# Writing the weights' low halves over their raw pieces: eight slots for high halves, splits up to six pieces ahead

## The chip, the cores and the metric

The kernel runs on one core of a Trainium2 chip. The metric is the device time of one execution in microseconds (us), the median of several runs. Besides the timed runs there is one execution under the hardware profiler, and every row below is from that one.

## The reference

Two layers of a streaming encoder trunk over 256 positions of width 2048, all in float32. Each layer adds three sub-layers to x, each between two RMSNorms:

```python
x = x + rmsnorm(hybrid_mixer(rmsnorm(x, g[0]), ...), g[1])   # w_in (2048 x 5,000-odd), attention of 16 heads, w_out
x = x + rmsnorm(memory_xattn(rmsnorm(x, g[2]), mem_n, wq_x, wkv_x, wo_x), g[3])
x = x + rmsnorm(conv_ffn(rmsnorm(x, g[4]), w_up, conv_w, conv_b, w_down), g[5])   # w_up 2048 x 8192, w_down 4096 x 2048
```

In the mixer, one part of the projection by w_in is low-rank: `cq` (512 columns) and `ckv` (256 columns and 32 for the rotary key) are each normalized and then multiplied by `w_uq` and `w_ukv` to give queries, keys and values of six heads.

## The kernel before

**The stream of pieces.** All weights of both layers are laid out as one stream of 688 pieces, 344 a layer, each [128 partitions x 1024 float32], 512 KB. A piece is loaded by SP's DMA queue into one of eight slots of `raw`. For TensorE, which is given float32r operands, each piece is split in two parts whose sum is the float32 value: ScalarE (ACT) copies `raw` into `w_hi`, rounded to float32r (`split_hi`, L983), and VectorE (DVE) writes `w_lo = raw - w_hi` (`split_lo`, L1299). TensorE (PE) then multiplies hi by hi, lo by hi and hi by lo into PSUM. `w_hi` and `w_lo` have four slots each (`SPL = 4`). The activations are split likewise (`h_t`, `c_t`, `o_t` and others, by ACT at L991 and DVE at L1331).

**What waits for what.** The semaphores are `landed[slot]` (a load is there), `hi_ready`, `lo_ready` (a split's two halves) and `split_free` (PE has used a piece). ACT's split of piece p waits for the landing and for PE having used piece p - 4. SP's load of piece p + 8 waits for `lo_ready` of piece p, that is until DVE has read the raw piece for the last time. PE's first matmul of a piece waits for `lo_ready` of it.

**The order is written out by hand.** `layer_steps` lists, for the first 152 pieces of a layer and the start of the up-projection, steps such as ("mm", p), ("evac", group), ("latent", "scale"), ("split", q). PE, ACT and DVE each walk through this one list in order and do their part of each step; after the steps of ("mm", p) stands ("split", p + 4). Up- and down-projection are loops with a split for each piece. So an engine that is held at a split is held for all that follows on it.

**The pieces of a layer.** 0 to 7 are `cq` (2 x 512 columns wide), 8 to 15 `ckv` (2 x 288: only 576 columns of the piece are split and multiplied), 16 to 23 `vbf` (2 x 262), 24 to 31 `vb`, 32 and 33 `uqa`, 34 to 37 `small` (the last columns of w_uq and w_ukv; 128 columns), 38 `ukv0`, 39 `ukv1`, 40 to 47 `va`, then 40 pieces of transposed q and k, 32 of w_out, 32 of the cross-attention, 128 of the up- and 64 of the down-projection. A group's result leaves PSUM by its ("evac", group) after its last piece; the groups alternate between two pairs of PSUM banks, so PE's first matmul of a group waits until ACT has emptied the group before the last one.

**The latent chain.** After piece 15 ACT sums the squares of `cq` and `ckv`; after piece 17 DVE computes their rstd; after piece 19 ACT scales them; after piece 20 DVE turns the rotary key; after piece 23 PE transposes two tiles (`latent_T` 0 and 1, L863) into two of four rotating banks, ACT and DVE split them into `c_t`; after piece 24 PE transposes `latent_T` 2, 3 and 4, and number 3 waits for DVE's `c_t` of number 0, which frees its bank. In layer 0 alone DVE also makes six `ind` tiles (L1485) for the bias of the heads of group A in between, and PE multiplies them.

## Time and profile before

| | |
|---|---|
| runs, us | 2049.18, 2048.83, 2047.91; median 2048.83 |
| the profiled execution, us | 2053.52, its span 2051.7 |
| PE busy | 1997.4 us, 97% of the span |
| DVE, ACT busy | 1384.1 us (67%), 1082.1 us (53%) |
| the weights' loads | 688 of 512 KB; DMA engines busy for them 52.2% of the span |
| granted TensorE clock, mean | 0.988 of full speed |

The profiled execution is 1.8 us longer than its span (what lies around the first and the last instruction) and 4.7 us longer than the median of the runs. Busy times count an engine's instructions only; what is left of PE's span, 54.3 us, is idle time: about 14 us of it lie behind its last matmul, and 9.3 us before its third group at the start.

### The profile page before, as it was taken

The numbers are of one execution on the slowest core, as the hardware profiler recorded it, in microseconds if no ns is written. First come the engines' busy times: TensorE is split into PE (matmuls) and PEld (weight loads), VectorE is DVE, ScalarE is ACT, GpSimd is POOL, SyncE is SP. The second block draws the span as 40 slices with busy tenths as digits, with TensorE's granted clock in tenths as the row PEclk, the third lists the DMA queues.
The fourth block names the chain that finished last, engine by engine and source line by source line (L and its number), as shares of the span: only waits on it lengthen the run. The fifth ranks groups of instructions, "written<-read, shape, count | busy, mean of one in ns | idle before, by whom it ended". The sixth has DMA issues, their size and how long they took to land.

```text
span 2051.7 us, 31077 instructions
## 1 busy us (share of the span) xinstructions
PE 1997.4 (97%) x10772; PEld 1710.6 (83%) x10772; DVE 1384.1 (67%) x2141; ACT 1082.1 (53%) x1682; POOL 169.2 (8%) x191
## 2 busy tenths in 40 slices
PE   8999999998999999999989999999989999999997
PEld 6788888887888888888878888788878888888885
DVE  6757676767777777744466576768577777777454
ACT  5665555645555555444456555565555555554442
POOL 0010000000112212100000000000002212211000
PEclk9999999999999999999999999999999999999999
DMA  7664446453555555565547444555445555556552
GB/s 276 219 211 147 163 147 242 176 175 134 178 195 190 182 196 187 183 225 192 192 168 242 165 146 164 186 212 193 149 143 185 186 193 193 181 196 210 193 192 82
DMA packets 104472, 379.00 MB, mean 185 GB/s; under 512 B 12032, under 2 KB 12672, under 8 KB 103040
## 3 DMA queue, kind: packets, MB, share of 16 engines
q1 hardware_dynamic: 101392, 365.11, 52.2%
q10 hardware_dynamic: 2416, 11.14, 1.5%
q0 software_dynamic: 576, 1.57, 0.3%
q8 instruction: 56, 0.92, 0.2%
q14 instruction: 32, 0.26, 0.0%
HBM read 374.90 MB, written 2.88 MB: 184 GB/s over the span
## 4 chain that ended last, share of the span: by engine, by line
PE 94%; DVE 3%; ACT 1%; issue 1%; DMA 0%; SPq 0%; DVEq 0%; ACTq 0%
PE ps L733 23%; PE ps L675 13%; PE ps L677 13%; PE ps L676 13%; PE ps L735 12%; PE ps L688 9%; PE ps L690 5%; PE ps L639 1%; DVE w_lo L1299 1%; DVE x L1443 1%; PE ps L916 1%; PE ps L901 0%; PE ps L904 0%; ACT w_hi L983 0%; PE ps L854 0%
## 5 line engine op out<-in xcount | busy, mean ns | idle before, releaser
L1299 DVE TENSOR_TENSOR w_lo<-raw,w_hi 128x1024 fp32r<-128x1024 f32 (+2 forms) x688 | 816.9, 1191 | 515.8 <-ACT w_hi L983 510.7
L983 ACT ACTIVATE w_hi<-raw 128x1024 fp32r<-128x1024 f32 (+2 forms) x688 | 706.0, 1031 | 493.6 <-PE ps L677 241.0
L733 PE MATMUL ps<-h_t,w_hi 128*128 128x512 f32 x2048 | 716.0, 396 | 4.1 <-DVE h_t L1331 2.4
L735 PE MATMUL ps<-h_t,w_lo 128*128 128x256 f32 x2048 | 569.2, 278 | 0.0
L733 PEld LDWEIGHTS ps<-h_t,w_hi 128*128 128x128 f32 x2048 | 385.9, 188 | 94.3 <-issue 5.2
L735 PEld LDWEIGHTS ps<-h_t,w_lo 128*128 128x128 f32 x2048 | 386.4, 189 | 0.0
L688 PE MATMUL ps<-h_t,w_hi 128*128 128x512 f32 x768 | 275.5, 401 | 0.0
L1787 POOL TENSOR_SCALAR up_c<-up_u,cw 128x256 f32<-128x256 f32 x128 | 125.8, 995 | 1202.0 <-DVE up_u L1682 1202.0
L690 PE MATMUL ps<-h_t,w_lo 128*128 128x256 f32 x768 | 215.2, 280 | 0.0
L675 PE MATMUL ps<-w_hi,act_t 128*128 128x512 f32 x512 | 199.2, 389 | 0.0
L677 PE MATMUL ps<-w_hi,act_t 128*128 128x512 f32 x512 | 199.2, 389 | 0.0
L676 PE MATMUL ps<-w_lo,act_t 128*128 128x512 f32 x512 | 199.2, 389 | 0.0
L688 PEld LDWEIGHTS ps<-h_t,w_hi 128*128 128x128 f32 x768 | 144.2, 188 | 33.6 <-issue 0.7
L690 PEld LDWEIGHTS ps<-h_t,w_lo 128*128 128x128 f32 x768 | 145.1, 189 | 0.3
L675 PE MATMUL ps<-w_hi,h_t 128*128 128x512 f32 (+2 forms) x320 | 117.9, 369 | 3.3 <-DVE w_lo L1299 2.1
L676 PE MATMUL ps<-w_lo,h_t 128*128 128x512 f32 (+2 forms) x320 | 113.7, 355 | 0.0
L677 PE MATMUL ps<-w_hi,h_t 128*128 128x512 f32 (+2 forms) x320 | 113.7, 355 | 0.0
L677 PEld LDWEIGHTS ps<-w_hi,act_t 128*128 128x128 f32 x512 | 96.1, 188 | 20.1
L675 PEld LDWEIGHTS ps<-w_hi,act_t 128*128 128x128 f32 x512 | 96.1, 188 | 20.0
L676 PEld LDWEIGHTS ps<-w_lo,act_t 128*128 128x128 f32 x512 | 96.1, 188 | 19.7
L675 PE MATMUL ps<-w_hi,o_t 128*128 128x512 f32 x256 | 102.9, 402 | 3.0 <-DVE o_t L1331 3.0
L677 PE MATMUL ps<-w_hi,o_t 128*128 128x512 f32 x256 | 100.2, 391 | 0.0
(277 smaller groups left out, 2311.4 us busy)
## 6 DMA issues: line engine op xcount, KB each, us to landing
raw<-stream SPq DMA_DIRECT2D x688, 512.0 KB, 4.0
gain_a<-gains_in ACTq DMA_DIRECT2D x4, 1024.0 KB, 6.6
m_nat<-mem_in ACTq DMA_DIRECT2D x2, 2048.0 KB, 10.6
x<-x_in SPq DMA_DIRECT2D x4, 512.0 KB, 8.1
gain_f<-gains_in ACTq DMA_DIRECT2D x2, 1024.0 KB, 7.7
out<-x SPq DMA_DIRECT2D x4, 512.0 KB, 2.8
bias_hbm<-bias_raw POOLq DMA_DIRECT2D x4, 128.0 KB, 5.1
bias<-bias_hbm POOLq DMA_DIRECT2D x4, 128.0 KB, 7.1
```

What stands on the lines that cost most here:

```text
L639: mm = pe.transpose(b[:, kk * SEQ + tb * P:kk * SEQ + (tb + 1) * P], x[:, tb, (2 * i + kk) * P:(2 * i + kk + 1) * P], ident[:])
L675: pe.matmul(dst, s_hi, hi[:, j, :], start=f, stop=False, skip_group_check=True)
L676: pe.matmul(dst, s_hi, lo[:, j, :], start=False, stop=False, skip_group_check=True)
L677: mm = pe.matmul(dst, s_lo, hi[:, j, :], start=False, stop=e, skip_group_check=True)
L688: pe.matmul(dst, hi[:, j, nt * P:(nt + 1) * P], src[:, c, :, :], start=f, stop=False, skip_group_check=True)
L690: mm = pe.matmul(dst[:, SEQ:2 * SEQ], lo[:, j, nt * P:(nt + 1) * P], src[:, c, 0, :], start=False, stop=e, skip_group_check=True)
L733: pe.matmul(dst, hi[:, cc, nt * P:(nt + 1) * P], h_t[:, c, :, :], start=(c == 0), stop=False, skip_group_check=True)
L735: mm = pe.matmul(dst[:, SEQ:2 * SEQ], lo[:, cc, nt * P:(nt + 1) * P], h_t[:, c, 0, :], start=False, stop=(c == KC - 1), skip_group_check=True)
L916: mm = pe.transpose(b[:, t * P:(t + 1) * P], s_sb[:, slot, o:o + P], ident[:])
L983: act.activation(w_hi[:, slot, 0:width], raw[:, rslot, 0:width], ACT.Copy).then_inc(hi_ready, 1)
L1299: dve.tensor_tensor(w_lo[:, slot, 0:width], raw[:, rslot, 0:width], w_hi[:, slot, 0:width].bitcast(F32), ALU.subtract).then_inc(lo_ready, 1)
L1787: ins = pool.tensor_scalar(up_c[:, nt, :], up_u[:, nt, :], cw[:, 4 * nt + 2:4 * nt + 3], cw[:, 4 * nt + 3:4 * nt + 4], ALU.mult, ALU.add)
```

## The change

Eight slots for `w_hi` take the 32 KB of each partition that four slots of `w_hi` and four of `w_lo` took, and `w_lo` lies at the address of `raw`: DVE writes a piece's low half over the raw piece that it reads in the same instruction. Since the slot of `raw` is then in use until PE has multiplied the piece, SP's load of piece p + 8 waits for `used`, PE's count of used pieces (the old `split_free` under another name and without its start value of 4), instead of `lo_ready` of piece p. ACT's split no longer waits for PE: a landed piece is free to be split, for the load before it has waited already. And the splits stand further ahead in the order: ("split", p + 4) for the first 12 pieces of layer 0, p + 5 up to piece 39, p + 6 from there on and in all of layer 1, so that two steps, after pieces 12 and 40 of layer 0, hold two splits.

```diff
-SPL = 4
+AHEAD = 6
+
+def splits_after(layer, p):
+    if layer > 0:
+        return [p + AHEAD]
+    def target(q):
+        return 3 if q < 0 else q + (4 if q < 12 else 5 if q < 40 else AHEAD)
+    return list(range(target(p - 1) + 1, target(p) + 1))
...
         if p < P_UP - 1:
-            steps.append(("split", p + SPL))
+            steps += [("split", q) for q in splits_after(layer, p)]
...
         raw = sb("raw", [P, RAW, PW], 0)
-        w_hi = sb("w_hi", [P, SPL, PW], 32 * K, F32R)
-        w_lo = sb("w_lo", [P, SPL, PW], 48 * K, F32R)
+        w_hi = sb("w_hi", [P, RAW, PW], 32 * K, F32R)
+        w_lo = sb("w_lo", [P, RAW, PW], 0, F32R)
...
-                    sp.wait_ge(lo_ready, r * RAW + (j + 1 - RAW))
+                    sp.wait_ge(used, r * RAW + (j + 1 - RAW))
                     sp.dma_start(raw[:, j, :], stream[r * RAW + j]).then_inc(landed[j], 16)
...
-            pe.sem_inc(split_free, SPL)
...
-            def split_hi(slot, rslot, landed_count, piece_count, width=PW):
-                act.wait_ge(landed[rslot], landed_count)
-                act.wait_ge(split_free, piece_count)
-                act.activation(w_hi[:, slot, 0:width], raw[:, rslot, 0:width], ACT.Copy).then_inc(hi_ready, 1)
+            def split_hi(slot, landed_count, width=PW):
+                act.wait_ge(landed[slot], landed_count)
+                act.activation(w_hi[:, slot, 0:width], raw[:, slot, 0:width], ACT.Copy).then_inc(hi_ready, 1)
...
-            def split_lo(slot, rslot, count, width=PW):
+            def split_lo(slot, count, width=PW):
                 dve.wait_ge(hi_ready, count)
-                dve.tensor_tensor(w_lo[:, slot, 0:width], raw[:, rslot, 0:width],
+                dve.tensor_tensor(w_lo[:, slot, 0:width], raw[:, slot, 0:width],
                                   w_hi[:, slot, 0:width].bitcast(F32), ALU.subtract).then_inc(lo_ready, 1)
```

The rest of the diff replaces `p % SPL` by `p % RAW`, `SPL` by `AHEAD` and `split_free` by `used` wherever they stand.

Two places of the written order are shown before and after. The first is DVE in layer 0, between the latent chain's rstd (whose last instruction stands just ahead of these rows) and the `c_t` of `latent_T` 0. Before:

```order
L1299 TENSOR_TENSOR w_lo<-raw,w_hi 128x524 [waits dve_step,hi_ready]
L1299 TENSOR_TENSOR w_lo<-raw,w_hi 128x524 [waits hi_ready] x2
L1503 TENSOR_TENSOR kr<-ckv,trig 128x2x16 [waits setup_act,acc_free1]
L1504 TENSOR_TENSOR rope_b<-ckv,trig 128x2x16
L1505 TENSOR_TENSOR kr<-ckv,trig 128x2x16
L1506 TENSOR_TENSOR rope_c<-ckv,trig 128x2x16
L1507 TENSOR_TENSOR kr<-kr,rope_b 128x2x16 [waits dve_step]
L1508 TENSOR_TENSOR kr<-kr,rope_c 128x2x16
L1299 TENSOR_TENSOR w_lo<-raw,w_hi 128x1024 [waits hi_ready,dve_step]
L1485 TENSOR_TENSOR ind<-past_edge,pos 128x2048 [waits bank_done]
L1299 TENSOR_TENSOR w_lo<-raw,w_hi 128x1024 [waits hi_ready] x2
L1331 SCALAR_TENSOR_TENSOR c_t<-ps,cols,c_t 128x256 [waits tsplit_hi]
```

After, one narrow split later (the piece split first is now 22, not 21; its row is left out here), and up to the row just ahead of the same `c_t`:

```order
L1303 TENSOR_TENSOR w_lo<-raw,w_hi 128x524 [waits hi_ready]
L1303 TENSOR_TENSOR w_lo<-raw,w_hi 128x1024 [waits hi_ready]
L1506 TENSOR_TENSOR kr<-ckv,trig 128x2x16 [waits setup_act,acc_free1]
L1507 TENSOR_TENSOR rope_b<-ckv,trig 128x2x16
L1508 TENSOR_TENSOR kr<-ckv,trig 128x2x16
L1509 TENSOR_TENSOR rope_c<-ckv,trig 128x2x16
L1510 TENSOR_TENSOR kr<-kr,rope_b 128x2x16 [waits dve_step]
L1511 TENSOR_TENSOR kr<-kr,rope_c 128x2x16
L1303 TENSOR_TENSOR w_lo<-raw,w_hi 128x1024 [waits hi_ready,dve_step]
L1488 TENSOR_TENSOR ind<-past_edge,pos 128x2048 [waits bank_done]
L1303 TENSOR_TENSOR w_lo<-raw,w_hi 128x1024 [waits hi_ready] x2
```

There are six splits between the same two points in both, but before they are those of pieces 21 to 26, three narrow and three wide, and after those of 22 to 27, two narrow and four wide. In layer 1 they are those of pieces 21 to 26 before and 23 to 28 after, one narrow and five wide.

The second is ACT in layer 1 around the `small` group, from the second half of the evacuation of `uqa` (after piece 33) to that of `small` (after piece 37). Before:

```order
L1132 ACTIVATE q_nat<-ps 128x512
L983 ACTIVATE w_hi<-raw 128x128 [waits split_free,landed5]
L983 ACTIVATE w_hi<-raw 128x1024 [waits split_free,landed6]
L983 ACTIVATE w_hi<-raw 128x1024 [waits split_free,landed7]
L983 ACTIVATE w_hi<-raw 128x1024 [waits split_free,landed0]
L1132 ACTIVATE q_nat<-ps 128x64 [waits split_free]
```

After:

```order
L1136 ACTIVATE q_nat<-ps 128x512
L989 ACTIVATE w_hi<-raw 128x1024 [waits landed7]
L989 ACTIVATE w_hi<-raw 128x1024 [waits landed0]
L989 ACTIVATE w_hi<-raw 128x1024 [waits landed1]
L989 ACTIVATE w_hi<-raw 128x1024 [waits landed2]
L1136 ACTIVATE q_nat<-ps 128x64 [waits used]
```

The four splits are those of pieces 37 to 40 before and 39 to 42 after, and the last of them waits for a load that SP issues when PE has used piece 34.

## Rows read from the trace of the kernel before

**Rows 1.** The page: its first line and busy times (in us) by engine.

```profile
span 2051.7 us, 31077 instructions
...
PE 1997.4 (97%) x10772; PEld 1710.6 (83%) x10772; DVE 1384.1 (67%) x2141; ACT 1082.1 (53%) x1682; POOL 169.2 (8%) x191
```

**Rows 2.** Waits of TensorE (PE): us in total, times, longest.

```profile
PE ps L675 <- DVE w_lo L1299: 2.1, 2, 1.5
...
PE ps L863 <- DVE c_t L1331: 1.1, 1, 1.1
```

**Rows 3.** Waits of ACT's high-half splits: us in total, times, longest.

```profile
ACT w_hi L983 <- DMA raw<-stream: 3.1, 3, 1.5
```

**Rows 4.** PE by time in layer 0: start, us, what [idle before <-releaser].

```profile
65.53 0.39 PE L675 MATMUL ps<-w_hi,h_t 128*128 128x262 f32 x1 [1.49 <-DVE w_lo L1299]
...
75.85 0.80 PE L863 MATMUL ps<-ident,ckv 128*128 128x128 f32 x4 [1.11 <-DVE c_t L1331]
```

**Rows 5.** DVE by time in layer 0, same columns.

```profile
64.77 1.32 DVE L1299 TENSOR_TENSOR w_lo<-raw,w_hi 128x524 fp32r<-128x524 f32 x2
67.42 0.70 DVE L1299 TENSOR_TENSOR w_lo<-raw,w_hi 128x524 fp32r<-128x524 f32 x1 [1.33 <-ACT w_hi L983]
...
69.22 1.23 DVE L1299 TENSOR_TENSOR w_lo<-raw,w_hi 128x1024 fp32r<-128x1024 f32 x1 [0.35 <-ACT w_hi L983]
...
72.56 2.36 DVE L1299 TENSOR_TENSOR w_lo<-raw,w_hi 128x1024 fp32r<-128x1024 f32 x2
74.83 1.26 DVE L1331 SCALAR_TENSOR_TENSOR c_t<-ps,cols,c_t 128x256 fp32r<-128x256 f32 x3
```

**Rows 6.** ACT by time in layer 0.

```profile
66.77 0.62 ACT L983 ACTIVATE w_hi<-raw 128x524 fp32r<-128x524 f32 x1
```

**Rows 7.** PE by time in layer 1.

```profile
1084.41 0.39 PE L675 MATMUL ps<-w_hi,h_t 128*128 128x262 f32 x1 [0.56 <-DVE w_lo L1299]
...
1092.53 0.60 PE L863 MATMUL ps<-ident,ckv 128*128 128x128 f32 x4
```

**Rows 8.** DVE by time in layer 1.

```profile
1083.65 1.32 DVE L1299 TENSOR_TENSOR w_lo<-raw,w_hi 128x524 fp32r<-128x524 f32 x2
1086.30 0.70 DVE L1299 TENSOR_TENSOR w_lo<-raw,w_hi 128x524 fp32r<-128x524 f32 x1 [1.33 <-ACT w_hi L983]
...
1087.78 3.50 DVE L1299 TENSOR_TENSOR w_lo<-raw,w_hi 128x1024 fp32r<-128x1024 f32 x3
1091.19 1.26 DVE L1331 SCALAR_TENSOR_TENSOR c_t<-ps,cols,c_t 128x256 fp32r<-128x256 f32 x3
```

**Rows 9.** ACT by time in layer 1.

```profile
1085.64 3.47 ACT L983 ACTIVATE w_hi<-raw 128x524 fp32r<-128x524 f32 x4
...
1120.61 2.01 ACT L983 ACTIVATE w_hi<-raw 128x1024 fp32r<-128x1024 f32 x2 [0.28 <-PE ps L677]
1122.53 0.20 ACT L1132 ACTIVATE q_nat<-ps 128x64 f32<-128x64 f32 x1
...
1122.89 0.29 ACT L1132 ACTIVATE vc<-ps 128x128 f32<-128x128 f32 x1
```

**Rows 10.** First matmul of piece 39 of layer 1.

```profile
1124.58 0.39 PE L675 MATMUL ps<-w_hi,c_t 128*128 128x512 f32 x1
```

**Rows 11.** Windows: us, busy us (instructions) by engine, granted clock, DMA share, GB/s.

```profile
103.24:115.94 12.70, 12.70 (x62) 11.04 (x61) 7.51 (x18) 8.37 (x20) 4.46 (x9) 0.73 1.00 298
646.00:680.00 34.00, 34.00 (x198) 29.73 (x197) 24.41 (x28) 20.40 (x21) 5.91 (x6) 1.00 0.59 194
1117.80:1127.30 9.50, 9.50 (x62) 8.52 (x61) 6.97 (x17) 8.27 (x20) 0.00 (x0) 1.00 0.88 282
```

**Rows 12.** Loads of raw, issue to landing, whole program, by its line.

```profile
DMA to landing us min/median/max: 3.0/4.0/12.8
```

**Rows 13.** The same, loads issued near 1116 to 1124 us.

```profile
DMA to landing us min/median/max: 4.4/5.1/6.0
```

**Rows 14.** The same, near 100 to 120 us.

```profile
DMA to landing us min/median/max: 3.4/5.8/10.3
```

More of the change, by code:

```diff
@@ L239, in layer_steps @@
         if p < P_UP - 1:
-            steps.append(("split", p + SPL))
-    steps += [("upd", 1, 0), ("upd", 1, 1), ("h3", 0), ("split", P_UP - 1 + SPL), ("upd", 1, 2)]
+            steps += [("split", q) for q in splits_after(layer, p)]
+    steps += [("upd", 1, 0), ("upd", 1, 1), ("h3", 0), ("split", P_UP - 1 + AHEAD), ("upd", 1, 2)]
     for i in range(8):
@@ L252, in layer_steps @@
         if i > 0:
-            steps.append(("split", P_UP + i - 1 + SPL))
+            steps.append(("split", P_UP + i - 1 + AHEAD))
         steps.append(("mm", P_UP + i))
-    steps += [("R", "h3"), ("split", P_UP + 7 + SPL)]
+    steps += [("R", "h3"), ("split", P_UP + 7 + AHEAD)]
     return steps
@@ L704, in w_in_piece @@
                     if kind == "T":
-                        mm = t_mm(gi, p % SPL, h_t, range(4 * j, 4 * j + 4), j == 0, j == n - 1)
+                        mm = t_mm(gi, p % RAW, h_t, range(4 * j, 4 * j + 4), j == 0, j == n - 1)
                     elif name == "uqa":
                         tile_ready(("latent_T", 2))
-                        mm = nat_mm(gi, p % SPL, 0, c_t, [2 * j, 2 * j + 1], 512, j == 0, j == 1)
+                        mm = nat_mm(gi, p % RAW, 0, c_t, [2 * j, 2 * j + 1], 512, j == 0, j == 1)
                     elif name == "small":
@@ L712, in w_in_piece @@
                         if j < 2:
-                            mm = nat_mm(gi, p % SPL, 0, c_t, [2 * j, 2 * j + 1], 64, j == 0, j == 1)
+                            mm = nat_mm(gi, p % RAW, 0, c_t, [2 * j, 2 * j + 1], 64, j == 0, j == 1)
                         else:
-                            mm = nat_mm(gi, p % SPL, 0, c_t, [2 + j], 128, j == 2, j == 3, col=64)
+                            mm = nat_mm(gi, p % RAW, 0, c_t, [2 + j], 128, j == 2, j == 3, col=64)
                     elif name.startswith("ukv"):
-                        mm = nat_mm(gi, p % SPL, 0, c_t, [4, 5], 512, True, True)
+                        mm = nat_mm(gi, p % RAW, 0, c_t, [4, 5], 512, True, True)
                     else:
@@ L758, in piece @@
                             tile_ready((tiles, 2 * j + t))
-                        t_mm(G_MEMK + k, p % SPL, src, range(4 * j, 4 * j + 4), j == 0, j == 3).then_inc(split_free, 1)
+                        t_mm(G_MEMK + k, p % RAW, src, range(4 * j, 4 * j + 4), j == 0, j == 3).then_inc(used, 1)
                     elif p < P_WO:
@@ L1240, in up_split @@
                 def up_split(i, half, j):
-                    split_dyn(P_UP + 8 * half + SPL, j, i, 16)
+                    split_dyn(P_UP + 8 * half + AHEAD, j, i, 16)
                 def up_tail(i, half, j):
@@ L1269, in _ @@
                 for j in range(8):
-                    split(P_DOWN + SPL + j)
+                    split(P_DOWN + AHEAD + j)
                     up_tail(UPG // 2 - 1, 1, j)
@@ L1275, in _ @@
                 for j in range(8, 16):
-                    split(P_DOWN + SPL + j)
+                    split(P_DOWN + AHEAD + j)
                 for k in range(1, 4):
@@ L1279, in _ @@
                     for j in range(16):
-                        if (k, j) != (3, 15) and (l < DEPTH - 1 or P_DOWN + 16 * k + SPL + j < NPIECES):
-                            split(P_DOWN + 16 * k + SPL + j)
+                        if (k, j) != (3, 15) and (l < DEPTH - 1 or P_DOWN + 16 * k + AHEAD + j < NPIECES):
+                            split(P_DOWN + 16 * k + AHEAD + j)
                 y_squares(G_DOWN + 3, 11)
@@ L1288, in _ @@
                     if step == ("h1", 0):
-                        split(NPIECES - 1 + SPL)
+                        split(NPIECES - 1 + AHEAD)
         @block.vector
@@ L1672, in up_split @@
                 def up_split(i, half, j):
-                    split_dyn(P_UP + 8 * half + SPL, j, i, 16)
+                    split_dyn(P_UP + 8 * half + AHEAD, j, i, 16)
                 def up_tail(i, half, j):
@@ L1713, in _ @@
                 for j in range(8):
-                    split(P_DOWN + SPL + j)
+                    split(P_DOWN + AHEAD + j)
                     up_tail(UPG // 2 - 1, 1, j)
                 for j in range(8, 16):
-                    split(P_DOWN + SPL + j)
+                    split(P_DOWN + AHEAD + j)
                 for k in range(1, 4):
@@ L1720, in _ @@
                     for j in range(16):
-                        if (k, j) != (3, 15) and (l < DEPTH - 1 or P_DOWN + 16 * k + SPL + j < NPIECES):
-                            split(P_DOWN + 16 * k + SPL + j)
+                        if (k, j) != (3, 15) and (l < DEPTH - 1 or P_DOWN + 16 * k + AHEAD + j < NPIECES):
+                            split(P_DOWN + 16 * k + AHEAD + j)
                 y_gain(G_DOWN + 3, 11, y_f, gain_f)
@@ L1730, in _ @@
                     if step == ("h1", 0) and l < DEPTH - 1:
-                        split(NPIECES - 1 + SPL)
+                        split(NPIECES - 1 + AHEAD)
         @block.gpsimd
```

41 lines of the change are left out of this document (19 added, 22 removed).

## The prediction, made before the changed kernel ran

> **What bounds the kernel now.** I read the page first. PE is busy for 1997.4 us of a span of 2051.7 [rows 1], so the most that any change to the weights' supply could give is the part of the 54.3 us of idle time that waits for weights. The waits of PE say how much that is: under the name of `w_lo` stand 2 waits, 2.1 us together [rows 2]. The timeline of PE gives their places: 1.49 us at 65.53 in layer 0 and 0.56 us at 1084.41 in layer 1, both in the narrow `vbf` pieces [rows 4, 7]. Everywhere else the splits are in time. The loads are in time too: ACT's splits have waited 3.1 us in all for a landing, 3 times [rows 3]. So the kernel is bound by PE, and the question is what happens at the few places where DVE and ACT are late.
>
> At the first of them I read PE and DVE side by side. PE gets its late piece at 65.53, and 10 us later it waits again, 1.11 us, for DVE's `c_t` [rows 2, 4]. DVE is the engine that is behind there: from 64.77 to that `c_t` at 74.83 it has two gaps, of 1.33 and 0.35 us, each ended by ACT [rows 5]. A late split and a late `c_t` are one queue on DVE, seen twice. In layer 1, which has no `ind` tiles, PE reaches the same transposes at 1092.53 without a wait [rows 7], while DVE begins `c_t` at 1091.19 [rows 8].
>
> **Loads tied to PE.** In the steady part PE does 198 matmuls in 34 us [rows 11]; 16 of them are a piece, so a piece takes 2.75 us. A load is now issued when PE has finished piece p - 8, and PE has seven pieces to go, 19.2 us. Against this stand a landing (median 4.0 us, longest 12.8 [rows 12]), a high half of about 1 us (the start-to-start time of two is 0.96 [rows 9]) and a low half of 1.14 us (three take 3.41 [rows 8]): 6 to 7 us, at the longest 15. So PE does not wait for a load in the steady part, and this edit costs nothing there; seven pieces of PE's work hide it. ACT meets its loads sooner: the split of p + 6 needs the load issued two pieces before, 5.5 us, more than the 4.0 of the median. In the narrow pieces and in `small` this margin is gone; that is the third term below. The removed wait of ACT for PE gives nothing by itself, as an early split is not what PE waits for.
>
> One rule of the Trainium skill bears on this margin. The rows show 3.0, 4.0 and 12.8 us for a load of 512 KB [rows 12]. The page "DMA: Bandwidth & Descriptors", section "Anatomy of one DMA — SWDGE (gpsimd) path", has a fixed cost of about 2 us and then 436 GB/s; for 512 KB that is an estimate of 3.2 us, near the shortest here and 0.8 below the median. By it the third term would be nothing and the sum 1.2 us instead of 1.8. It was fitted on another queue than SP's, and I go by the rows.
>
> **The slots and the in-place write.** The same 688 instructions of each engine with the same shapes; DVE still reads two operands and writes one. No row shows a subtraction whose output lies on its input. I bound it from both sides by the wide low half of before, 1.14 us, and 5% to either side of it (0.06 us): DVE, 67% busy [rows 1], hides that everywhere but in the two chains below, where 6 splits each make 0.7 us in all. I take no change.
>
> **Term 1, the latent chain of layer 0: 0.6 us later.** The first double split, after piece 12, shifts every later one by a piece. Before `c_t` DVE has still six splits after the rstd, but one narrow one has become wide. Step by step from the rows: the first two are the same as before and end at 66.1. Then it waits for ACT's next high half, which starts at 66.77 behind the scaling [rows 6]. This half was narrow, with 0.65 us until DVE began at 67.42; it is wide now, 0.95 with the same hand-over of 0.12, so DVE begins at 67.84, 0.42 later. The low half itself takes 1.14 instead of 0.62 (the start-to-start times), 0.52 more. The rotary key follows as before. The gap of 0.35 before 69.22 goes, as that high half is ready sooner in DVE's order. 0.42 + 0.52 - 0.35 = 0.59: `c_t` at 75.4 instead of 74.83. PE waited for this `c_t`, so its transposes come at 76.4 instead of 75.85. The stall of 1.49 us at 65.53 goes, as piece 21 is split before the rstd; but PE then only arrives earlier at the same `c_t` and waits longer there. It gives nothing back.
>
> **Term 2, the same in layer 1: 0.6 us later.** The order is two pieces ahead, so after the rstd come one narrow and five wide. DVE: narrow from 1083.65 to 1084.27, wide to 1085.4; then it waits for ACT, whose first high half behind the scaling starts at 1085.64 [rows 9] and is wide: 0.42 later than the 1086.30 of before, 1086.72. Wide 1.14 for 0.62, again 0.52 more; the rotary key; three wides as before. No gap is there to swallow it: `c_t` at 1091.19 + 0.94 = 1092.13. In layer 0 PE's transpose followed the start of `c_t` by 75.85 - 74.83 = 1.02 us, so here it can come at 1093.15 instead of 1092.53, 0.6 later. The 0.56 us of 1084.41 and some tenths beside it are again only time that PE arrives earlier with.
>
> **Term 3, `small` in layer 1: 0.6 us later.** ACT has between the evacuations of `uqa` and `small` now the splits of 39 to 42, and piece 42 is loaded when PE is done with piece 34. Piece 34 begins at 1117.8. The 62 matmuls from there to 1127.3 [rows 11] are two wide pieces of 2.75 and 36 short ones in the remaining 4.0 us, 0.11 each; a piece of 12 takes 1.3, so the load is issued at 1119.1 to 1119.2. Loads issued there took 4.4, 5.1 and 6.0 [rows 13]; I take the lowest, since loads bound to PE come less in bursts. It lands at 1123.6, its high half ends at 1124.55, and the evacuation of `small`, which takes 0.65 (1122.53 to the end of the row at 1122.89 [rows 9]), ends at 1125.2. PE needs that PSUM for piece 39 at 1124.58 [rows 10]: 0.6 us late. With the median of 5.1 it is 1.3, with 6.0 it is 2.2, with 3.7 nothing. What is queued behind the waiting split on ACT is the evacuation of `ukv0`, before which ACT has one more split; it needs to be done for piece 40, about 1.3 us after it was (1.28 us long), and that margin takes the shift. In layer 0 the same place has one piece less of advance, and PE is slow there: its granted clock is 0.73 over the window, 12.70 us for what takes 9.50 in layer 1 [rows 11]. I take nothing.
>
> **Sum.** 0.6 + 0.6 + 0.6 = 1.8 us. Against the profiled execution's own 2053.52 us this makes 2055.3; that execution is 4.7 above the median of the runs, so for the median I forecast 2048.83 + 1.8 = 2050.6 us. The bounds from the terms alone: term 1 from 0 to 1.0, term 2 from -1.1 (its removed stalls kept) to 1.0, term 3 from 0 to 2.2, that is 2047.7 to 2053.0. A difference of up to 0.2%, 4.1 us, is about what a measurement of this kernel cannot tell from none.
>
> **The rivals.**
> - *The removed stalls are kept* (20%). For it: they are the only waits for weights, 2.1 us, and DVE's gaps in both chains could take the wider splits if ACT were earlier. Against it: the gaps are ACT's scaling, which does not move. Time: 2048.8 - 2.1 = 2046.7.
> - *The clock changes its places* (12%). In layer 0 the window of `small` stands at 0.73 of the clock, in layer 1 at 1.00, for the same 62 matmuls; the difference is 3.2 us [rows 11]. The level of 1.2 GHz that is mixed into that 0.73 came after a stretch of short matmuls, without an idle gap of PE. If it goes away in layer 0: 2050.6 - 3.2 = 2047.4, and with the first rival 2043.5. If the wait of term 3 brings it to layer 1: 2053.8. Against both: PE's order and the lengths of its matmuls stay.
> - *Tied loads hold ACT for long* (slower, 10%). The mechanism is a long landing in front of the evacuation of `small`, in both layers. In layer 0 GpSimd's bias copies share the DMA engines there (share 1.00 [rows 11]) and loads took up to 10.3 us [rows 14]. Piece 41 is loaded when piece 33 is done, at 103.3. PE needs `small`'s PSUM 6.8 us after piece 34 begins in layer 1 (1117.8 to 1124.58), and 3.2 later at the clock of layer 0, at 113.2. With a landing of L the evacuation ends at 103.3 + L + 0.95 + 0.65, so PE waits from L = 8.3 on; at 10.3 it is 2.0 us. With 6.0 in layer 1 term 3 is 2.2, and the sum 1.2 + 2.0 + 2.2 = 5.4: 2054.2. With 6.0 in layer 1 it is slower by the bound from 9.0 in layer 0 on; with term 3 as I take it, from 10.6. Against it: the medians are 5.8 and 5.1 [rows 13, 14].
> - *The change doesn't act*: DVE is the late engine either way and the terms are noise, 2048.8. I count it into the main case, whose interval holds it.
>
> **How the numbers follow.** Main case (small, later by 0 to 4) 58%, the removed stalls kept 20%, clock 12%, held ACT 10%. The main case's own range is 2048.5 to 2053. Leaving out the last fifth at both ends: 2046.3 to 2054.2. Faster by over 0.2% (under 2044.7) needs the clock and the first rival together: 5%. Slower by over 0.2% (over 2052.9): held ACT 8%, a clock fall in layer 1 or term 3 at its top 7%, so 15%. The rest, 80%, is no change.
>
> **What would show it.** After the change PE should have no wait for `w_lo`, near 65.5 and near 1084; it should wait for `c_t` about 2.5 us in all near 76, 1 to 2 us near 1093 (this row is new), and about 0.6 us for the evacuation of `small` near 1125. ACT's splits should wait for landings often, with hundreds of us in total, and hardly for PE. If PE's wait for `c_t` in layer 0 is shorter than 1.1 us, term 1 is wrong; if the wait at 1093 is not there, term 2. What would make the whole wrong is a wait of PE for `w_lo` in the steady part, low halves of more than 1.2 us in the mean, or other stretches of low clock than those at the start, at 106 and behind the long waits.

## The result, and the profile after

The changed kernel takes 2057.23 us (median of 13 runs, 2053.47 to 2069.67), the kernel before 2049.84 us (13 runs, 2046.86 to 2060.77): ratio 1.003, 95% interval 1.0017 to 1.0044. It is slower, by 0.17 to 0.44%, where I had forecast 2050.6 us and no measurable change. A second series gave 1.0027 (1.0013 to 1.0042). The profiled execution took 2069.67 us.

The page's first line and its busy times:

```profile
span 2067.8 us, 30402 instructions
...
PE 2009.9 (97%) x10772; PEld 1716.1 (83%) x10772; DVE 1382.2 (67%) x2141; ACT 1074.8 (52%) x1682; POOL 168.7 (8%) x191
```

The waits that answer to [rows 2, 3] (us in total, times, longest):

```profile
PE ps L870 <- DVE c_t L1335: 4.5, 2, 2.5
PE ps L740 <- DVE w_lo L1303: 0.9, 1, 0.9
PE ps L682 <- ACT vc L1136: 0.7, 1, 0.7
ACT w_hi L989 <- DMA raw<-stream: 461.6, 345, 3.3
```

The 2.1 us that PE waited for `w_lo` in the narrow pieces are gone, as forecast (the 0.9 us under that name are at the first piece of the up-projection, where the kernel before waits 0.85 us too, under the name of `issue`). The wait for `c_t` has grown from 1.1 to 4.5 us, and there is a new wait for an evacuation in layer 1. By time on PE, for [rows 4, 7, 10]:

```profile
74.38 0.80 PE L870 MATMUL ps<-ident,ckv 128*128 128x128 f32 x4 [1.95 <-DVE c_t L1335]
1098.92 0.41 PE L870 MATMUL ps<-ident,ckv 128*128 128x128 f32 x2 [2.51 <-DVE c_t L1335]
1133.23 0.50 PE L682 MATMUL ps<-w_hi,c_t 128*128 128x512 f32 x1 [0.68 <-ACT vc L1136]
```

PE's *busy* time has also grown, by 12.5 us for the same 10772 matmuls, and that can't be a wait. The windows (us of the window; busy and count; granted clock; DMA share; GB/s) show two kinds of slower work:

```profile
646.00:680.00 34.00, 34.00 (x195) 1.00 0.53 187
1680.00:1714.00 34.00, 34.00 (x194) 1.00 0.55 185
75.70:79.10 3.40, 3.40 (x9) 0.50 0.00 0
1099.70:1103.10 3.40, 3.40 (x10) 0.50 0.00 0
1103.20:1106.60 3.40, 3.40 (x17) 1.00 0.49 152
```

Behind each wait for `c_t` stands a stretch of 3.4 us with the clock at 0.50 (1.2 GHz), in which PE does 9 or 10 matmuls where the next 3.4 us hold 17. And the first two rows hold 195 and 194 matmuls where [rows 11] had 198, at a full clock: the up-projection ran at another pace, in both layers, from its first loop piece to its last. Starts of pieces are 2.827 us apart in the mean where they were 2.773 before; 120 pieces in two layers make that 12.8 us. The question for the experiments was which of these the change causes.

### The profile page after: what moved, and what is told of

Read it like the earlier page. It is cut to its first block, busy times and chain, and to the rows that moved or that the text cites. A ratio compares the mean times of both kernels' runs of the same rounds, so it can differ in the third digit from the quotient of the medians.

```text
span 2067.8 us, 30402 instructions
## 1 busy us (share of the span) xinstructions
PE 2009.9 (97%) x10772; PEld 1716.1 (83%) x10772; DVE 1382.2 (67%) x2141; ACT 1074.8 (52%) x1682; POOL 168.7 (8%) x191
## 4 chain that ended last, share of the span: by engine, by line
PE 93%; DVE 4%; ACT 2%; DMA 1%; issue 1%; SPq 0%; DVEq 0%; ACTq 0%
PE ps L740 23%; PE ps L682 13%; PE ps L684 13%; PE ps L683 13%; PE ps L742 12%; PE ps L695 9%; PE ps L697 5%; PE ps L646 1%; DVE w_lo L1303 1%; DVE x L1446 1%; PE ps L923 0%; DMA raw<-stream 0%; ACT w_hi L989 0%; PE ps L908 0%; PE ps L911 0%
## 5 line engine op out<-in xcount | busy, mean ns | idle before, releaser
L989 ACT ACTIVATE w_hi<-raw 128x1024 fp32r<-128x1024 f32 (+2 forms) x688 | 701.0, 1031 | 463.0 <-DMA raw<-stream 461.6
L740 PE MATMUL ps<-h_t,w_hi 128*128 128x512 f32 x2048 | 729.2, 401 | 4.1 <-DVE h_t L1335 2.4
L695 PE MATMUL ps<-h_t,w_hi 128*128 128x512 f32 x768 | 275.5, 401 | 0.0
```

Source lines behind the costliest of these rows:

```text
L695: pe.matmul(dst, hi[:, j, nt * P:(nt + 1) * P], src[:, c, :, :], start=f, stop=False, skip_group_check=True)
L740: pe.matmul(dst, hi[:, cc, nt * P:(nt + 1) * P], h_t[:, c, :, :], start=(c == 0), stop=False, skip_group_check=True)
L989: act.activation(w_hi[:, slot, 0:width], raw[:, slot, 0:width], ACT.Copy).then_inc(hi_ready, 1)
```

## The experiments

Run-to-run differences here are as large as the effect, so besides whole times I use one sum by stage that turned out steady: PE's time from the first matmul of piece 16 to that of piece 32 (`vbf` and `vb`) in both layers, plus that from piece 32 to piece 40 (`uqa` to `ukv1`) in layer 1, read from PE's timeline. I call it **the sum**; it holds all three terms of the prediction. Layer 0's pieces 32 to 39 are left out: they took 15.9 to 19.1 us in the profiles, by the half clock that the kernel before has there too; what the change does to them is said under e6. "First c_t" is DVE's start of it, counted from PE's start on piece 16. All executions in one table (the first two rows are the kernel before):

| profile | us | layer 0, 16-31 | layer 1, 16-31 | layer 1, 32-39 | the sum | first c_t, layer 1 | pace, layers 0 and 1 |
|---|---|---|---|---|---|---|---|
| before, first | 2053.52 | 42.47 | 36.22 | 14.98 | 93.67 | 15.10 | 2.773, 2.773 |
| before, again (e12) | 2055.93 | 42.49 | 36.21 | 14.95 | 93.65 | 15.09 | 2.773, 2.827 |
| change, first | 2069.67 | 44.64 | 39.43 | 16.00 | 100.07 | 17.19 | 2.827, 2.827 |
| change (e1) | 2057.95 | 43.05 | 37.07 | 16.14 | 96.26 | 16.44 | 2.827, 2.773 |
| change (e8) | 2061.89 | 44.41 | 39.05 | 16.12 | 99.58 | 16.84 | 2.827, 2.773 |
| change (e13) | 2061.16 | 44.69 | 37.42 | 16.53 | 98.64 | 16.81 | 2.773, 2.827 |
| change (e14) | 2053.12 | 44.53 | 37.20 | 16.55 | 98.28 | 16.59 | 2.773, 2.773 |
| change (e15) | 2062.89 | 44.63 | 40.07 | 16.46 | 101.16 | 17.88 | 2.773, 2.827 |
| change (e16) | 2070.65 | 44.13 | 40.38 | 16.52 | 101.03 | 18.38 | 2.827, 2.827 |
| order of before (e2) | 2057.18 | 42.38 | 36.22 | 14.96 | 93.56 | 15.10 | 2.827, 2.773 |
| advance from piece 40 (e3) | 2054.90 | 42.36 | 36.21 | 14.96 | 93.53 | 15.09 | 2.773, 2.827 |
| loads tied only (e4) | 2047.59 | 42.45 | 36.20 | 14.95 | 93.60 | 15.09 | 2.773, 2.773 |
| layer 1 five ahead (e5) | 2050.57 | 43.06 | 36.66 | 14.96 | 94.68 | 16.03 | 2.773, 2.773 |
| four ahead at `small` (e6) | 2068.75 | 44.66 | 39.44 | 14.96 | 99.06 | 17.20 | 2.827, 2.827 |
| tapered (e7) | 2056.03 | 41.84 | 35.09 | 18.17 | 95.10 | 14.27 | 2.773, 2.827 |
| c_t 3 times more (e9) | 2058.56 | 42.49 | 40.07 | 14.99 | 97.55 | 15.09 | 2.827, 2.773 |
| c_t 6 times more (e10) | 2058.57 | 42.46 | 43.53 | 14.98 | 100.97 | 15.10 | 2.773, 2.773 |
| tapered, ind moved (e11) | 2053.45 | 40.33 | 35.09 | 16.54 | 91.96 | 14.28 | 2.827, 2.773 |

### Which part of the change costs: e1 to e4

**e1, the change again.** No edit.

> The changed kernel once more, unaltered. Leaves nothing out. The question is what its slower up-projection (2.827 us a piece in the first profile, 2.773 in the kernel before, 120 pieces in each of two layers, 6.4 us a layer) is tied to. Theory A (a state of single executions, whatever the kernel): the profile shows 2.773 in one layer or both at least half the time, and the spread of the timed runs has steps of about 6.4 us; the fastest runs are 2053 to 2055. Theory B (tied to the changed buffers or loads): 2.82 or more in both layers again, and the change costs 12.8 us that something else gives back in part. By both: ratio 1.002 to 1.004 and PE's waits for c_t about 2.0 and 2.5 us near 74 and 1099.

Ratio 1.0027 (1.0013 to 1.0042), the sum 96.26, one layer at 2.827 and one at 2.773, waits for `c_t` of 1.95 and 1.76 us, and no half clock behind either. So the pace is no fixed property of the changed kernel.

**e2, the order of before.**

```diff
-AHEAD = 6
+AHEAD = 4
-    if layer > 0:
-        return [p + AHEAD]
     def target(q):
-        return 3 if q < 0 else q + (4 if q < 12 else 5 if q < 40 else AHEAD)
+        return q + 4
```

> The changed buffers, in-place write and tied loads with the order of before (each split four pieces ahead throughout). Leaves nothing out. Theory A (the order alone costs, through the latent chain and the clock behind it): ratio 1.000 (0.999 to 1.001), c_t waited for 1.1 us in layer 0 and not in layer 1, w_lo 1.5 and 0.6 as before. Theory B (buffers or tied loads cost): ratio 1.002 to 1.004 as with the whole change, and 2.82 us a piece in the up-projection.

Ratio 0.9992 (0.9975 to 1.0009), the sum 93.56, waits as before. New slots, in-place write and tied loads together cost nothing that shows: the sum differs by 0.1 us, and the interval of the whole time ends at 1.0009.

**e3, the advance only from piece 40 on.**

```diff
     def target(q):
-        return 3 if q < 0 else q + (4 if q < 12 else 5 if q < 40 else AHEAD)
+        if q < 0:
+            return 5 if layer else 3
+        return max(q + (4 if q < 40 else AHEAD), 5 if layer else 3)
```

> The change with the further advance put off: four pieces ahead up to piece 39 in both layers, six from piece 40 on. Leaves nothing out. Theory A: ratio 1.000 (0.999 to 1.001), c_t waits as before (1.1 and none), no wait for the evacuation in front of ukv0 near 1125. Theory B, or if the six ahead of the long part cost something: 1.002 to 1.004.

Ratio 1.0002 (0.9986 to 1.0017), the sum 93.53. Six ahead in the long part of both layers gives nothing, and the one steady cost by stage is 0.3 us in pieces 88 to 151 of layer 1 (212.40 for 212.07 us); the loss is made by the order in front of piece 40.

**e4, the kernel before with tied loads.**

```diff
-                    sp.wait_ge(lo_ready, r * RAW + (j + 1 - RAW))
+                    sp.wait_ge(split_free, r * RAW + (j + 1 - RAW) + SPL)
```

> The kernel before with one edit: SP's load of piece p + 8 waits for PE having used piece p instead of for the low half of p. Buffers and order are those of before. Leaves nothing out. Theory A: ratio 1.000 (0.999 to 1.001); with four ahead every load has 3 to 4 pieces (8 to 11 us) until its split. Theory B in the form that tied loads disturb PE's pace: 1.002 to 1.004 and 2.82 us a piece; if B is the in-place write or the slots: 1.000 here and 1.002 to 1.004 in the run with the order of before.

Ratio 1.0007 (0.999 to 1.0023), the sum 93.60 and both layers at 2.773: theory A for this edit too. The interval alone would let 0.2% stand; the sum does not. These four settle that the order costs, and not the buffers.

### Which step of the order: e5 and e6

**e5, layer 1 five ahead up to piece 39.**

```diff
-    if layer > 0:
-        return [p + AHEAD]
     def target(q):
-        return 3 if q < 0 else q + (4 if q < 12 else 5 if q < 40 else AHEAD)
+        if q < 0:
+            return 5 if layer else 3
+        return q + (5 if layer and q < 40 else 4 if q < 12 else 5 if q < 40 else AHEAD)
```

> The change with layer 1 only five ahead up to piece 39, as layer 0 is. Leaves nothing out. Read by stage in the profile, layer 1. Theory A (ACT's wide split of piece 24, which at six ahead stands in front of the latent scaling and waits for its load, makes the chain later beyond the wider splits): from the first vbf piece to DVE's first c_t 15.1 to 15.7 us, against 15.1 in the kernel before and 16.4 and 17.2 in the two profiles of the change; PE's wait for c_t there 1 us or less, no stretch of half clock behind it. Theory B (the wider splits alone): 16.0 or more still. The pieces from uqa to ukv1: A and B 15.0 to 15.4, since piece 41 now stands where 42 did, against 15.0 before and 16.0 and 16.1 with the change. Whole time: ratio 1.000 to 1.002.

The first `c_t` of layer 1 comes at 16.03, the number of theory B, which is 0.93 later than before: almost exactly the 0.94 that I had worked out for the wider splits. In the change it comes 1.34 to 3.28 later. The difference is on ACT. In the change (first profile), then in e5, ACT by time in layer 1, from the last split in front of the latent scaling (L1161):

```profile
1088.43 1.06 ACT L989 ACTIVATE w_hi<-raw 128x1024 fp32r<-128x1024 f32 x1 [1.58 <-DMA raw<-stream]
1089.40 1.32 ACT L1161 ACTIVATE cq<-cq,rst 128x512 f32<-128x512 f32 x2
```

```profile
1077.45 0.64 ACT L989 ACTIVATE w_hi<-raw 128x524 fp32r<-128x524 f32 x1 [0.96 <-DMA raw<-stream]
1079.14 1.35 ACT L1161 ACTIVATE cq<-cq,rst 128x512 f32<-128x512 f32 x2 [1.04 <-DVEq L1499]
```

At six ahead the wide split of piece 24 stands in front of the scaling and waits for its load, which SP issues only when PE has used piece 16. ACT gets to the scaling when that load lets it, and has no idle time in front of it. At five ahead ACT is early and waits 1.04 us for the rstd instead. e1 is the one profile of the change in which the load of piece 24 came in time for the scaling:

```profile
1085.83 1.34 ACT L1161 ACTIVATE cq<-cq,rst 128x512 f32<-128x512 f32 x2 [0.27 <-DVEq L1499]
```

There the rstd itself was 0.4 us later than before, since the squares on ACT had stood behind the split of piece 20 and its wait of 1.28 us for a landing. So both theories held in part: the wider splits are 0.9 us, the landings in front of the squares and of the scaling 0.4 to 2.3 on top. PE's wait for `c_t` in layer 1 of e5 was 1.35 us instead of 1.8 to 3.3, and no half clock followed. The ratio, 1.0022 (1.0005 to 1.0039), is at the top of what I expected and above; the profile, with the sum at 94.68, is on the low side, for it has no half clock in layer 0 either, where seven of the nine profiles with this order have it.

**e6, four ahead around `small`.**

```diff
-    if layer > 0:
-        return [p + AHEAD]
     def target(q):
-        return 3 if q < 0 else q + (4 if q < 12 else 5 if q < 40 else AHEAD)
+        if q < 0:
+            return 5 if layer else 3
+        if layer:
+            return q + AHEAD if q < 26 else max(31, q + 4) if q < 40 else q + AHEAD
+        return q + (4 if q < 12 else 5 if q < 40 else AHEAD)
```

> The change with layer 1 back to four ahead for pieces 28 to 39 only, so that ACT's splits around small are those of the order before. Leaves nothing out. Theory A (the third term is a landing in front of an evacuation): the pieces from uqa to ukv1 of layer 1 take 15.0 us as before instead of 16.0 to 16.1, and everything else stays as with the change: c_t waited for 1.9 to 2.5 us in layer 1. Theory B (that time is lost to something else, such as the clock): 16 again. Whole time about 1 us less than with the change, ratio 1.002 to 1.003.

Pieces 32 to 39 of layer 1 are back at 14.96 us, and the rest is as with the change (17.20 to the first `c_t`, half clock behind both waits). Theory A: the third term is what it was said to be, with 1.0 us or more instead of 0.6. The ratio, 1.0035 (1.0017 to 1.0053), does not tell this kernel from the change. In the first profile of the change ACT does, ahead of the evacuation of `small`:

```profile
1129.25 1.06 ACT L989 ACTIVATE w_hi<-raw 128x1024 fp32r<-128x1024 f32 x1 [0.49 <-DMA raw<-stream]
1131.57 1.06 ACT L989 ACTIVATE w_hi<-raw 128x1024 fp32r<-128x1024 f32 x1 [1.25 <-DMA raw<-stream]
```

Two landings in a row are late, not only the last.

The same wait stands in layer 0, where I had taken nothing. In e8:

```profile
111.67 0.50 PE L682 MATMUL ps<-w_hi,c_t 128*128 128x512 f32 x1 [1.37 <-ACT vc L1136]
```

In the five profiles of the change without half clock over `small` of layer 0 (e1, e8, e14, e15, e16) it is 0.80 to 1.69 us long, and pieces 32 to 39 take 17.05 to 17.95 us; with the order of before and no half clock there (e3, e4, e9) they take 15.94 to 15.97. Where half clock stands there (the first profile and e13) PE has no such wait, and the time is that of the kernel before at as much half clock: 19.13 and 17.53 for 19.13 and 17.52. The mean over all profiles hardly moves, 17.66 for 17.31 us in the seven with the order of before, as four of these have the half clock and only two of the change; whether that share differs by more than chance is not shown.

### What a wait for c_t costs: e9 and e10

**e9 and e10, c_t made late in the kernel before**, by repeating DVE's low half of the first transpose of layer 1, 3 and 6 times:

```diff
                     dve.wait_ge(tsplit_hi, TSPLIT[(l, item)] + 1)
+                    if item == ("latent_T", 0) and l == 1:
+                        for _ in range(3):
+                            st.done(lo_tile(*tsplit_job(item, layer), bank(l, item)))
```

> The kernel before with DVE's low half of latent_T 0 in layer 1 made three times more than needed (each with a wait for its own end) before the one that counts: c_t comes 2.5 us later, nothing else is changed, nothing is left out. PE comes to the transposes 0.3 us after c_t allows it in the kernel before, so it waits 2.2 us, about as long as in layer 1 of the change (1.9 to 2.5). Theory A (such a wait is what brings the 3.4 us of half clock that three of four profiles of the change show behind it): pieces 24 to 31 of layer 1 take 22.86 + 2.2 = 25.1 us, or with a stretch of half clock 26.8. Theory B (the half clock there comes from something else in the change): 25.1 in every case, no half clock near the wait.

> The same with six extra low halves: c_t comes 5.1 us later, nothing is left out. PE waits 4.8 us in layer 1. Theory A: a stretch of half clock behind the wait, certain if a longer wait makes it likelier; pieces 24 to 31 of layer 1 take 27.7 plus 1.7 for each stretch of 3.4 us, so 29.4 or 31.1. Theory B: 27.7. Whole time by A 6 to 8 us more than the kernel before (ratio 1.003 to 1.004), by B 4.8 (1.0023).

PE's row with the wait in e9, and the window at half clock behind it (busy time and count of PE, PEld, DVE, ACT and POOL, then the granted clock, DMA share, GB/s):

```profile
1096.41 0.41 PE L863 MATMUL ps<-ident,ckv 128*128 128x128 f32 x2 [2.03 <-DVE c_t L1331]
```

```profile
1097.80:1101.00 3.20, 3.20 (x9) 2.42 (x9) 2.55 (x6) 0.70 (x2) 0.00 (x0) 0.50 0.51 164
```

The same of e10:

```profile
1093.92 0.66 PE L863 MATMUL ps<-ident,ckv 128*128 128x128 f32 x2 [4.77 <-DVE c_t L1331]
```

```profile
1092.30:1098.90 6.60, 4.98 (x13) 4.04 (x14) 5.52 (x12) 1.63 (x3) 0.00 (x0) 0.50 0.23 79
```

Behind these windows the clock is back at 1.00, and 3.4 us hold 17 matmuls in both. Theory A. In a kernel that has nothing of the change in it, one stretch of 3.4 us at half clock comes with a wait of 2.0 us and two with one of 4.8 us, the first of which begins while PE still waits. Pieces 24 to 31 take 26.71 us in e9, the case with a stretch, and 30.17 in e10, between the two numbers of theory A. Pieces 16 to 31 take 3.85 us more for the 2.03 us wait and 7.3 more for the 4.77: the wait, and 1.8 and 2.5 us on top. The ratios are 1.0029 (1.0012 to 1.0045) and 1.0048 (1.0029 to 1.0068). The case is not certain for a wait of this size, though. In the seven profiles of the change the wait in layer 0 is 1.95 us each time, and half clock follows in six (not in e1; of e5 and e6, with the same order in layer 0, it follows in e6 only); in layer 1 it follows the waits of 2.16, 2.51, 3.20 and 3.28 us and not those of 1.76, 1.90 and 2.12. The waits of 1.1 us for `c_t` in layer 0 of the kernel before, of e2, e3 and e4 never had it. One rule of the Trainium skill bears on this: the page "TensorE: Matmul & The Clock Gate", section "HAM oscillation — how this bites in real kernels", has waits for data throw TensorE to half clock and prices that at half of the time spent so. By it a stretch of 3.4 us costs an estimate of 1.7 us, and the traces are near it. In layer 0 pieces 16 to 31 take 43.05 us in e1 and 44.13 to 44.69 in the six profiles with a stretch, 1.1 to 1.6 more behind the same wait. In layer 1 they take 35.3 us besides PE's wait in the three profiles without a stretch (e1, e13, e14) and 36.9 to 37.1 in the four with one, 1.6 to 1.8 more. The mean over the ten stretches is 1.5 us.

### Whether the order can be made better: e7 and e11

**e7, a tapered order**, which splits piece 21 before the rstd and leaves two narrow and three wide splits between the rstd and the first `c_t`:

```diff
-    if layer > 0:
-        return [p + AHEAD]
     def target(q):
-        return 3 if q < 0 else q + (4 if q < 12 else 5 if q < 40 else AHEAD)
+        start = 5 if layer else 3
+        if q < 0:
+            return start
+        return max(start, q + (4 if q < 12 else 5 if q < 19 else 4 if q < 40 else AHEAD))
```

> Buffers of the change, another order, the same in both layers: four ahead up to piece 11, five for 12 to 18, four again for 19 to 39 and six from 40 on, so that piece 21 is split before the rstd and only five splits, two narrow and three wide, stand between the rstd and the first c_t. Leaves nothing out. Theory A (a late w_lo and a late c_t are one queue, and both stalls go if fewer splits stand between rstd and c_t): no wait for w_lo in the narrow pieces, c_t waited for 0.5 us or less in both layers, pieces 16 to 31 take 41.0 to 41.8 us in layer 0 (42.4 before, 43.1 and 44.6 with the change) and 35.0 to 35.5 in layer 1 (36.2 before, 37.1 and 39.4). Theory B (DVE is simply full there): the time of before in both. Whole time: 1 to 2 us less than before, ratio 0.999 to 1.000, which the timed runs hardly tell.

No wait for `w_lo` in the narrow pieces, none for `c_t` in layer 1; pieces 16 to 31 take 0.6 us less than before in layer 0 and 1.1 less in layer 1. The wait for `c_t` in layer 0 stayed at 1.1 us, which I had expected at 0.5 or less: PE arrives earlier by as much as `c_t` does. And the gain was given back: pieces 32 to 39 of layer 1 took 18.17 us, with half clock over the short matmuls of `small`, where neither profile of the kernel before has any. Ratio 0.9998 (0.9979 to 1.0018).

**e11, the same, and three ind tiles moved behind the latent chain of layer 0.**

```diff
-            at(9 + 4 * i, ("ind", i))
-            at(12 + 4 * i, ("bias", i))
+            at((9, 13, 17, 24, 28, 31)[i], ("ind", i))
+            at((12, 16, 20, 27, 30, 33)[i], ("bias", i))
```

> The tapered order (five ahead for pieces 12 to 18, four for 19 to 39, six from 40 on) with the fourth to sixth ind tiles of layer 0 moved behind the latent chain: from after pieces 21, 25, 29 to after 24, 28, 31, and their bias products from after 24, 28, 32 to after 27, 30, 33. Leaves nothing out. If the last wait for c_t in layer 0 (1.1 us, DVE's fault by 2.2 us of one ind tile) is all that is left there: no c_t wait of more than 0.2 us in either layer, pieces 16 to 31 take 40.7 to 41.0 us in layer 0 (42.4 before, 41.8 tapered) and 35.1 in layer 1 (36.2 before). Whole time: 2.5 to 3 us less than the kernel before at equal clock and pace, ratio 0.998 to 1.000. If the moved tiles are waited for instead, the gain of layer 0 is back to 0.6.

No wait for `c_t` is left in either layer. DVE by time in layer 0, where the kernel before had an `ind` tile of 2.29 us, from 70.36, among the wide splits of [rows 5]:

```profile
66.77 3.50 DVE L1304 TENSOR_TENSOR w_lo<-raw,w_hi 128x1024 fp32r<-128x1024 f32 x3 [1.79 <-ACT w_hi L990]
70.37 1.27 DVE L1336 SCALAR_TENSOR_TENSOR c_t<-ps,cols,c_t 128x256 fp32r<-128x256 f32 x3
```

Pieces 16 to 31 of layer 0 take 40.33 us, 2.1 less than before and under the 40.7 that I had expected at the least, those of layer 1 35.09, 1.1 less. Half clock came over `small` again (16.54 us), and the sum is 91.96, 1.7 under that of the kernel before. It is the best of the orders tried by that sum; the whole time does not tell it from the kernel before, ratio 0.9998 (0.9981 to 1.0016).

### Whether the pace of the up-projection comes with the change: e8, e12 to e16

No edits: e8 and e13 to e16 are the change, e12 the kernel before.

> One more look at the unaltered change, for the share of slow layers in the up-projection (3 of 4 layers at 2.83 us a piece in its two profiles, 3 of 8 in the profiles of the other kernels). If the pace is a matter of chance alike for all: one layer in two or three slow. If it is tied to the change: layer 0 slow again. Pieces 16 to 31: 43.0 to 44.7 in layer 0, 37.0 to 39.5 in layer 1.

> The kernel before, unaltered, once more for its profile: the pace of its up-projection in each layer (both 2.773 us a piece in its first profile) and its stretches of half clock. If the pace is a matter of chance alike for all kernels, each layer is slow once in two or three; the rest by stage as in the first profile, with no half clock behind the latent chain.

> The unaltered change, one of four more looks. So far its profiles had layer 0 slow in the up-projection 3 times of 3, layer 1 once of 3; all other kernels 4 of 11 in either layer. By chance alone each look has a slow layer 0 in about half the cases, so four looks all slow would be 1 in 16; tied to the change, layer 0 is slow in all of them. Pieces 16 to 39 of both layers together 4.5 to 6.5 us longer than in the two profiles of the kernel before if stretches of half clock follow the waits for c_t, 2.5 to 3.5 if not.

> The unaltered change, second of four looks: the pace of both layers of the up-projection (2.773 or 2.827 us a piece), and half clock behind the waits for c_t, as said for the first.

> The unaltered change, third of four looks: the pace of both layers of the up-projection (2.773 or 2.827 us a piece), and half clock behind the waits for c_t, as said for the first.

> The unaltered change, fourth of four looks: the pace of both layers of the up-projection (2.773 or 2.827 us a piece), and half clock behind the waits for c_t, as said for the first.

e12 shows both paces in one execution of the kernel before; the windows of [rows 11], in layer 0 and in layer 1:

```profile
646.00:680.00 34.00, 34.00 (x198) 1.00 0.63 202
1680.00:1714.00 34.00, 34.00 (x195) 1.00 0.63 200
```

and in e14 the same windows of the change hold 198 and 199 matmuls, the quicker pace in both layers. Of the four profiles e13 to e16 one has a slow layer 0 (e16), where a tie to the change would have had four.

Over the seven profiles of the change 8 of 14 layers ran at 2.827 us a piece, over the eleven of the other kernels 8 of 22: nothing that tells them apart. The timed runs of the first series say the same. Those of the kernel before stand in steps 6 to 7 us apart, 7 near 2048, 5 near 2055 and 1 at 2060.8; those of the change 8 near 2055, 4 near 2062 and 1 at 2069.7. The shares are alike, and each step is some 7 us higher. Between series the share does move, for one and the same kernel: of the timed runs of the kernel before, 18 of 35 lie at 2047 to 2051 us and none at 2060 or above in the series of e1 to e4, 3 of 29 and 12 of 29 in that of e5 and e6. So the pace is not the change: within a series it falls as if by chance, at the first loop piece of a layer, and is worth 6.4 us a layer; 12.8 of the 16.15 us between the first two profiles were this. What sets it, and its share in a series, is open. Ratios are taken within a series only.

With one layer at each pace in both, e8 and e12 compare directly: 2061.89 against 2055.93 us, 5.96 more, where the sum has 5.93 (99.58 against 93.65). That the two agree so closely is luck: the stages outside the sum differ by up to 1.5 us either way, which cancels here. With 6.4 us taken off for each slower layer, though, the spans of the seven profiles of the change are 2049.7 to 2056.0 us, median 2053.6, and those of the first, e12, e2, e3 and e4 2045.7 to 2051.7, median 2047.7: 5.9 us again, by a count that leaves no stage out.

In the expectation of e13, pieces 16 to 39 of both layers should take 4.5 to 6.5 us more than in the two profiles of the kernel before with stretches of half clock, and 2.5 to 3.5 without. Against the mean of these two it is 4.2, 3.4, 6.2 and 7.0 us in e13 to e16. e13 and e14 have a stretch behind one wait only, e15 and e16 behind both, so the two ranges were too narrow on both sides.

## Why the prediction was wrong

**What held.** The slots and the in-place write cost nothing: a wide low half lasts 1224 to 1228 ns in the mean in the profiles of both kernels (1225 in the first one), where I had bounded the difference at 5% to either side. Tied loads cost nothing in the steady part (e4, e2, e3), and ACT's splits wait for landings 461.6 us in all. The narrow stalls went and gave nothing back, since PE waits longer for `c_t` instead. **Term 1** was right: DVE's first `c_t` of layer 0, counted from piece 16, comes at 21.06 instead of 20.49, 0.57 later for the 0.59 forecast, and in e1 pieces 16 to 31 take 0.58 us more. PE's wait was 1.95 us each time, where I had said about 2.5: the 1.49 us of the removed stall did not all go into it, for PE waits 1.0 and 0.7 us for two `ind` tiles in the change, where it waited 0.43 for one before.

**Where it failed: term 2.** Its sum of durations was exact for an order in which no landing holds the squares or the scaling (0.93 in e5 for 0.94). But I carried over from the trace of before that ACT's high halves come right behind the scaling, and that the scaling "does not move". The splits of pieces 20 to 24, six ahead and with loads tied to narrow pieces of 1.5 us each, now stand in front of the squares and of the scaling on ACT and wait there for their landings. I had done this sum for `small` and had left it out for the chain, though the rule was in my own text: "In the narrow pieces and in `small` this margin is gone". `c_t` came 1.34 to 3.28 us late in layer 1 instead of 0.94, and pieces 16 to 31 there took 0.84 us more where it was earliest (e1), 1.0 and 1.2 in e14 and e13, for the 0.6 of the term.

**Where it failed most: the clock behind the wait.** The prediction priced a wait at its own length. I had a rival for half clock, but placed it at `small`; behind the waits for `c_t`, which I had forecast, I took none. It stood in layer 0 in six profiles of seven and in layer 1 in four, at 1.5 us each in the mean: 2.2 us a profile (10 stretches in 7 profiles), more than the whole forecast. The last sentence of the prediction exempted low clock "behind the long waits" from what would make it wrong; it should have had a price.

**Term 3** was in the right place and too small: pieces 32 to 39 of layer 1 took 1.0 to 1.6 us more, not 0.6. In four profiles PE waits 0.68 to 0.89 us there, as two splits in front of the evacuation wait for their landings; in e13, e14 and e16 it has no such wait, and half clock stands in its place (1.6 us more). **In layer 0**, at the same place, the prediction put the term at nothing; it is 1.1 to 2.0 us where no half clock stands over `small`, and nothing where it does.

**The sum.** Over the seven profiles of the change the sum is 96.3 to 101.2, median 99.58, against 93.5 to 93.7 in the five profiles with the order of before in front of piece 40 (e2, e3, e4, e12 and the first): 5.9 us, where I had 1.8. The waits themselves make 2.6 us in e1, which has no half clock in these stages, and 4.4 in e15 (7.5 less two stretches of 1.6); the clock makes the rest. The rival of kept stalls is out: their time went to the longer wait for `c_t`. The one of loads that hold ACT named a mechanism that is there, at `small` of both layers, but not the other place where it acts, in front of the squares and the scaling; the one of the clock named the right cost in the wrong place. As I gave them, neither was the likeliest case, and 2057 us stood outside the range. The number 2057 has some chance in it too. The 2048.83 us that I started from was the median of three runs of the lowest step, that of all 13 is 2049.84, and the medians of the two kernels lie 7.4 us apart in the first series and 5.4 in the second, where the stages have 5.9.

## What to carry to other kernels

Where an order of work is moved ahead, redo for each chain with a deadline the whole row of instructions in front of it on every engine, waits for loads included: an early split that waits for its load is a late everything-else behind it. Price a new wait of TensorE of about 2 us at its length and some 1.5 us for the half clock that may follow: here it did behind 10 of 14 waits of 1.8 to 3.3 us. And where single executions differ by more than the change, compare stages that repeat to a tenth of a microsecond, and take several profiles before a difference in another stage is put down to the change: here the largest one, 12.8 us, was not its doing.

## What the hardware showed unexpectedly

- The same loop of the up-projection runs at 2.773 or 2.827 us a piece at a granted clock of 1.00, and keeps its pace through all 120 pieces of a layer. Start to start, matmuls alternate between 232 and 115 ns in the mean in one and between 236 and 117 in the other. Both occur in one execution of one kernel (e12).
- The median from issue to landing is 4.0 to 4.1 us in the four profiles without tied loads ([rows 12], e9, e10 and e12) and 3.2 to 3.4 in thirteen of the fourteen with them. In e2, whose loads are tied in the same way, it is 4.3. So tied loads alone do not make it shorter, and what does is open. The page "DMA: Bandwidth & Descriptors" of the Trainium skill, section "Anatomy of one DMA — SWDGE (gpsimd) path", gives the estimate of 3.2 us that the prediction had set aside for the 4.0 of the trace; it fits the thirteen profiles, on SP's queue, and not e2.
- Half clock came over the short matmuls of `small` in layer 1 in five of the eleven profiles whose order in layer 1 is not that of before (e7, e11, e13, e14, e16), and in none of the seven with the order of before in front of piece 40. Why it goes there was not tried further.
